# Second norm of a long single-core kernel: turns of the tokens directly behind the modulation's picks, rounding tile by tile, and gate rows behind two heads' queries

## What is computed

```python
# first block, 512 tokens
x = x + concat([y_pool, y_mlstm, y_attn]) @ w_out
x = x + mem_cross_attn(rmsnorm(x, norm_mem_g), mem, ca_wq, ca_wkv, ca_wo)   # the second norm; q = hn @ ca_wq, 4 heads of 128
x = x + ec_moe(rmsnorm(x, norm_ffn_g), router_w, expert_w_gu, expert_w_down)
# second block
shift, scale, gate = split((silu(c) @ w_mod + b_mod)[:, None, :], 3)        # "the modulation"
shift_c, scale_c, _ = split(silu(c_ctx) @ w_mod + b_mod, 3)
h  = rmsnorm(x, norm_g) * (1 + scale) + shift
hc = rmsnorm(ctx, norm_g) * (1 + scale_c) + shift_c
...
x = x + gate * y
```

## Time and profile before

| | us |
|---|---|
| median of 3 runs | 1841.17 (1838.69 to 1841.96) |
| the profiled execution's own time | 1843.9 |
| its span, first to last instruction | 1842.0 |
| TensorE busy in the span | 1686.3 (92%) |
| VectorE, ScalarE, GpSimd busy | 585.0, 468.2, 268.5 |
| mean granted clock of TensorE | 0.989 |

### The profile page before, as it was taken

The page is one execution under the profiler, slowest core; times in us unless marked ns, Lnnn a source line. Parts: engine busy times, 40 slices in busy tenths (PEclk is TensorE's granted clock), DMA queues, the critical chain, the costliest instruction groups (busy, mean ns, idle before and its releaser), DMA issues.

```text
span 1842.0 us, 21089 instructions
## 1 busy us (share of the span) xinstructions
PE 1686.3 (92%) x8647; PEld 985.2 (53%) x8647; DVE 585.0 (32%) x1053; ACT 468.2 (25%) x865; POOL 268.5 (15%) x124
## 2 busy tenths in 40 slices
PE   7999999889898898898979979889899999999998
PEld 5897576653342432424324333243485458878876
DVE  4986784440110200202002020020266351260055
ACT  4456625310000100001000010010264432363232
POOL 0004411000000000000000000000140664116470
PEclk9999999989999999999999999999999999999999
DMA  9334045339999999999999999999901005203111
GB/s 334 134 128 126 1 160 234 121 149 430 427 428 428 429 429 428 429 429 429 428 429 428 428 428 430 429 427 429 383 1 46 1 6 121 92 31 113 68 76 46
DMA packets 65594, 484.19 MB, mean 263 GB/s; under 512 B 10268, under 2 KB 17909, under 8 KB 39807
## 3 DMA queue, kind: packets, MB, share of 16 engines
q1 hardware_dynamic: 65535, 483.36, 64.8%
HBM read 480.94 MB, written 2.41 MB: 262 GB/s over the span
## 4 chain that ended last, share of the span: by engine, by line
PE 72%; DMA 17%; DVE 6%; issue 2%; ACT 2%; POOL 0%; DVEq 0%; SPq 0%; ACTq 0%
PE psum L548 24%; PE psum L1859 17%; DMA ring<-in_expert_w_down 14%; PE psum L1879 7%; PE psum L1842 4%; PE psum L1888 3%; PE psum L2831 2%; PE psum L700 2%; PE psum L665 2%; PE psum L678 2%; DMA ring<-in_expert_w_gu 1%; PE psum L2515 1%; PE psum L2490 1%; PE psum L2499 1%; PE psum L864 1%
## 5 line engine op out<-in xcount | busy, mean ns | idle before, releaser
L1859 PE MATMUL psum<-ring,work_area 128*64 128x512 f32 x2048 | 448.3, 594 | 34.9 <-DMA ring<-in_expert_w_gu 27.1
L1859 PEld LDWEIGHTS psum<-ring,work_area 128*64 128x64 f32 x2048 | 147.8, 137 | 328.9 <-issue 276.9
L1879 PE MATMUL psum<-ring,work_area 128*64 128x512 f32 x1024 | 231.4, 606 | 18.1 <-DMA ring<-in_expert_w_down 16.0
L1949 DVE TENSOR_TENSOR work_area<-psum,work_area 128x512 f32<-128x512 f32 x32 | 20.6, 686 | 592.5 <-ACT work_area L1912 592.5
L1879 PEld LDWEIGHTS psum<-ring,work_area 128*64 128x64 f32 x1024 | 74.5, 139 | 163.9 <-issue 142.2
L2102 POOL TENSOR_TENSOR hn<-x_res,ring 128x1024 f32<-128x1024 f32 x3 | 9.0, 3012 | 1025.5 <-DVE x_res L1956 1025.5
L1912 ACT ACTIVATE work_area<-psum 128x512 f32<-128x512 f32 x32 | 17.4, 594 | 484.8 <-PE psum L1859 484.8
L2014 POOL TENSOR_TENSOR block_lo<-ring,part_hi 128x1024 fp32r<-128x1024 f32 x35 | 86.3, 2473 | 141.6 <-ACT part_hi L2007 141.2
L548 PE MATMUL psum<-h_hi,part_hi 128*128 128x512 f32 x240 | 93.7, 391 | 1.0 <-DVE hn L817 1.0
L1956 DVE TENSOR_TENSOR x_res<-psum,x_res 128x512 f32<-128x512 f32 x64 | 44.2, 691 | 156.9 <-PE psum L1888 156.9
L548 PE MATMUL psum<-h_hi,block_lo 128*128 128x512 f32 x240 | 93.4, 389 | 0.0
(11 more groups left out here) (485 smaller groups left out, 2719.6 us busy)
## 6 DMA issues: line engine op xcount, KB each, us to landing
ring<-in_expert_w_gu SPq DMA_DIRECT2D x128, 2048.0 KB, 27.5
ring<-in_expert_w_down SPq DMA_DIRECT2D x64, 2048.0 KB, 22.4
ring<-in_w_in SPq DMA_DIRECT2D x12, 2048.0 KB, 8.8
extra<-in_w_mod SPq DMA_DIRECT2D x4, 1536.0 KB, 10.6
ring<-in_w_out SPq DMA_DIRECT2D x3, 2048.0 KB, 13.6
ring<-in_ca_wkv SPq DMA_DIRECT2D x2, 2048.0 KB, 12.8
hn<-in_w_mod SPq DMA_DIRECT2D x2, 1536.0 KB, 6.9
x_res<-in_x SPq DMA_DIRECT2D x2, 1024.0 KB, 13.5
```

Of the source, the lines that this page charges most:

```text
L1859: ins = pe.matmul(psum[h * 64:(h + 1) * 64, c, :], xsT[:, k, e * CAP:(e + 1) * CAP], w[:, (2 * c + h) * BANK:(2 * c + h + 1) * BANK], star ...
L1879: ins = pe.matmul(psum[n * 64:(n + 1) * 64, 6, :], hidT[b][:, j, h, :], w[:, j, n * BANK:(n + 1) * BANK], start=(q == 0 and j == 0), stop= ...
```

## The change

Four things move; no operation is added or removed.

1. The gate rows leave their place ahead of the picks. The new `gate_row_pe` stands in `qca_pe` ahead of `ctx_pe`, behind the queries of two heads, and `gate_row_act` stands at the same place of ScalarE's drains.
2. On ScalarE, the rounding of the turned groups of the first tile goes ahead of the sum of squares of the third tile, and that of the second tile ahead of the fourth's.
3. On VectorE, the four rests of these groups go between the fourth tile's additions and its mean.
4. `g_gate_row` is taken from the banks later, so the picks and the turns use other banks, and the context's junk lies where it does not touch the gate's sums.

```diff
@@ add_norm, on_act
                 for t in range(T):
                     if arrived and t % 2 == 0:
                         act.wait_ge(arrived[t // 2], 16)
+                    if t in besides:
+                        besides[t]()
                     for g in groups[2 * t:2 * t + 2]:
                         B.drained(act, g)
                     act.activation(dst[:, t, :], src[:, t, :], ACT.Square, accum_out=ss[:, t:t + 1]).then_inc(squared, 1)
@@ add_norm, on_dve
                         B.release(dve.tensor_tensor(o, B.at(g), o, ALU.add), g)
+                    if t in besides_dve:
+                        besides_dve[t]()
 
                     dve.wait_ge(squared, turn[1] + t + 1)
@@ mod_pe
             pe.wait_ge(mod_added, KD)
-            pe.wait_ge(sem("gate_lin_in"), 16 * 2)
-            for j, g in enumerate(g_gate_row):
-                B.acquire(pe, g)
-                B.filled(product(g, B.at(g), [(ones, mod_total[:, 2 * D + j * BANK:2 * D + (j + 1) * BANK]),
-                                              (ones[0:1, :], gate_lin[j])]), g)
-
             pe.wait_ge(sem("pads"), 4)
...
+        def gate_row_pe():
+            pe.wait_ge(sem("gate_lin_in"), 16 * 2)
+            for j, g in enumerate(g_gate_row):
+                B.acquire(pe, g)
+                B.filled(product(g, B.at(g), [(ones, mod_total[:, 2 * D + j * BANK:2 * D + (j + 1) * BANK]),
+                                              (ones[0:1, :], gate_lin[j])]), g)
+
+        def gate_row_act():
             for j, g in enumerate(g_gate_row):
                 B.full(act, g)
                 B.release(copy(act, gate_row[:, j * BANK:(j + 1) * BANK], B.at(g)), g)
+
+        def mod_act():
             g = g_mod[0]
@@ banks
-        norm2_act, norm2_dve = add_norm(g_out1, x_sb, hn_ca, hn_mem)
-        g_gate_row = B.take(2)
+        norm2_act, norm2_dve = add_norm(g_out1, x_sb, hn_ca, hn_mem, besides={2: lambda: round_h2_act(range(0, 2)), 3: lambda: round_h2_act(range(2, 4))},
+                                        besides_dve={3: lambda: rest_of_h2_dve(range(0, 4))})
         g_mod = B.take(1)
         g_h2 = B.take(KD)
         g_modT = B.take(1)
...
-        ctx_junk = cut(W, 6656, 2, D)
+        ctx_junk = cut(W, 2048, 2, D)
         g_qca = B.take(2)
+        g_gate_row = B.take(2)
         g_ctx = B.take(4)
@@ qca_pe
                 if h == 2:
+                    gate_row_pe()
                     ctx_pe()
@@ qca_drain
                 if h == 2 and eng is act:
+                    gate_row_act()
                     ctx_drain_act()
@@ scalar
             mod_act()
-            round_h2_act()
+            round_h2_act(range(4, KD))
@@ vector
             norm2_dve()
-            rest_of_h2_dve()
+            rest_of_h2_dve(range(4, KD))
```

More of the change, by code:

```diff
@@ L468, in rms_rows, with add_norm @@
             return on_act, on_dve
-        def add_norm(groups, src, dst, mark, arrived=None):
+        def add_norm(groups, src, dst, mark, arrived=None, besides={}, besides_dve={}):
             squared, mean_ready, root_ready = sem("rows_squared"), sem("mean_ready"), sem("root_ready")
@@ L1202, in mod_pe @@
             B.filled(ins, g)
-        def mod_act():
+        def gate_row_pe():
[5 more added lines that the diff above has]
+        def gate_row_act():
             for j, g in enumerate(g_gate_row):
@@ L1581, in build, with round_h2_act, rest_of_h2_dve @@
         four_turns = lambda g: B.at(g).rearrange("p (k c) -> p k c", k=4)
-        def round_h2_act():
-            for i, g in enumerate(g_h2):
+        def round_h2_act(groups):
+            for i in groups:
+                g = g_h2[i]
                 B.full(act, g)
                 act.activation(tile_of(hq_hi, i), four_turns(g), ACT.Identity).then_inc(hT_rounded, 1)
-        def rest_of_h2_dve():
-            for i, g in enumerate(g_h2):
+        def rest_of_h2_dve(groups):
+            for i in groups:
+                g = g_h2[i]
                 dve.wait_ge(hT_rounded, T + i + 1)
```

## The result

The changed kernel is slower: 1847.16 us median against 1842.09 (14 runs each), a ratio of 1.0026 with a 95% interval of 1.0019 to 1.0032, or 4.8 us (0.0026 times 1842; the interval is 3.5 to 5.9 us). The forecast was 6.5 us more than a median of 1841.17 from three executions, which makes 1847.7; with 14 executions the median of before is 0.9 us higher. So the forecast time is met, but the forecast difference lies above the interval. The profiled execution has a span of 1845.3 us against 1842.0.

What follows compares the result with a forecast made beforehand. TensorE, busy 1686.3 of 1842.0 us, was taken to bound the kernel. Gate rows 4.1, terms 2 to 4 together 1.6 and clock 0.8 made +6.5 us, from 1841.2 to 1847.7; range 1843.6 to 1850.6.

Steps and rivals of the forecast that it cites:

- Term 1: Gate rows among queries and context turns, where TensorE has no idle time to cover them: +4.1 us.
- Term 2: In the norm, ScalarE's early roundings wait for TensorE's turns, delaying the third tile's squares: +3.6 us.
- Term 3: On VectorE, four rests stand ahead of the fourth tile's mean and delay it: +1.1 us.
- Term 4: The tail from the fourth tile's scaling to the first query shortens from 6.91 to 3.85 us: -3.0 us.
- Term 5: TensorE's clock low in holes: turns lose 0.8 us, queries lose 1.6 as before; +0.8, bounds -1.6 and +2.6.
- The terms past the stage: Behind the queries, the experts' stage starts later by the queries' delay, keeps its length and absorbs nothing.
- the last query "6 to 7 us later": Sign that the forecast is right: TensorE's last query before attention ends 6 to 7 us later.
- That the clock is low between and behind the holes: Expected low TensorE clock inside holes of 2.4, 4 and 1.4 us around the later tiles' turns.
- the dearer clock (1849.5): Rival: clock low through all turns and the queries' first 6.5 us, +8.3 us; chance 0.14.
- The first case of the rival within 0.2%: Low clock wholly in the holes, turns at full speed: +4.1 us; whole rival, no change to be told, chance 0.13.
- The one in which the early rests close the hole for nothing: Another case within 0.2%: hole ahead of queries closed, -2.4, beside gate rows +4.1: +1.7 us; whole rival's chance 0.13.

Runs made afterwards that it cites:

- e8: The reordered version (e4) with both gate rows moved behind two heads' queries; 1845.19 us against 1842.06 before, ratio 1.0020.
- e4: Changed kernel reordered: picks behind two tiles' turns, gate rows in TensorE's holes, four roundings before the fourth tile's squares, two early rests; 1838.59 us against 1842.17 before.
- e9: The reordered version (e4) with the gate rows and their copies left out altogether; 1839.00 us against 1842.44 before, ratio 0.9978.
- e2: Changed kernel with all four early roundings ahead of the fourth tile's squares, none ahead of the third's; 1842.94 us against 1842.17 before, ratio 1.0005.
- e1: Changed kernel with roundings and rests put back behind the fourth tile, so only the gate rows moved; 1845.98 us against 1842.17 before, ratio 1.0019.
- e12: Second profile of the unchanged kernel before; first query at 24.19 us and last drain at 49.61 us from the norm's first addition.
- e7: Changed kernel with the gate rows back in their old place ahead of the picks, roundings and rests still early; 1847.91 us against 1842.06 before.
- e3: Changed kernel with the gate rows in the holes behind the second and third tiles' turns; 1847.75 us against 1842.17 before, ratio 1.0032.
- e5: As e3, but ScalarE copies the picks ahead of the fourth tile's squares, removing a bank wait; 1843.88 us against 1842.06 before, ratio 1.0011.

## Why the prediction was right, by its own steps

The direction was right, and so was the place. The time (1847.16 for 1847.7) is nearer than the sum deserves: the difference is 4.8 us (3.5 to 5.9) where 6.5 were forecast, and a median of before that is 0.9 us higher than the three executions had it hides about half of that. In the profiled pair the last drain moved by 4.67 us, which can be set against the terms (against the second profile of before it is 3.3, with 0.7 in place of 2.2 for terms 2 to 4).

- **Term 1, gate rows, +4.1:** 4.11 (300.33 to 304.44), with nothing idle around them. e8 against e4, and the free gate rows of e4 against e9, show that it is the place and not the products.
- **Term 2, ScalarE's wait, +3.6:** 3.68 (13.84 against 10.16 from the norm's start). e2 takes it away alone and the first query comes 3.9 earlier.
- **Term 3, rests ahead of the mean, +1.1:** the scaling is 4.70 late (20.51 against 15.81 from the norm's start), less 3.68 leaves 1.02.
- **Term 4, the tail, -3.0:** 4.39 us (284.98 to 289.37) against 6.91, so -2.5. In it are the slow turns of term 5, for which I had put 0.8; they cost some 0.5 (4.39 less the 3.85 worked out).
- **Term 5, the clock, +0.8:** this term was mis-sized. I put 0.8 for the turns and left the queries' loss at 1.6. The turns did run at half clock, but the low stretch ended as the queries began (27.99 us with 4.11 of gate rows, 23.88 without, against 25.50 before): -1.6 for the queries and +0.5 for the turns, -1.1 in all, inside the bounds of -1.6 and +2.6. This accounts for the whole gap between 6.5 and 4.7: 4.1 for the gate rows, 2.2 for terms 2 to 4 with their slow turns, and -1.6 for the queries make 4.7.

One premise was wrong, though the sum did not rest on it: that the gate rows cost nothing in their old place because the other engines' chain passes them by. The chain of the kernel before (start, us, what) runs through their copies:

```profile
279.69 0.20 ACT small L488
279.89 0.98 ACT work_area L426 x2
280.87 0.48 ACT ring L426
281.35 0.50 ACT hq_hi L1586
281.85 0.02 issue
281.87 4.89 DVE hq_lo L1591 x8
```

The 0.98 us of copies stand between the fourth root and the roundings, and the rests and the first query hang on these; TensorE would not have let them start sooner either: its turns begin at 280.49, behind its own gate rows, which by the 0.69 us from a group's turns to ScalarE's reading puts the first rounding at 281.2. e1 measures it: the first query comes 1.0 us earlier without them. In the sum this gain sits in term 4, whose tail was worked out with the copies gone. So moving the gate rows alone costs 4.1 less 1.0, and e1 has 3.5 us (1.8 to 5.2).

The terms past the stage held too: 81.98 and 81.94 us up to the gather, an experts' stage of the same length. Of the signs, the last query "6 to 7 us later" came out at 4.8, for the same reason. That the clock is low between and behind the holes was right. What stays open is how often the clock falls inside the queries of either kernel: there are two profiles of each, which is too few.

Of the rivals, the dearer clock (1849.5) did not come: the queries ran at 1.00. The first case of the rival within 0.2% came by half: the low stretch fell ahead of the queries, as there, but the turns were slow all the same, and what was left, 4.8 us, stood clear of the noise. The one in which the early rests close the hole for nothing did not come, since ScalarE's wait was real; e4 shows what it would have needed: turns ahead of the picks, roundings only in ScalarE's gap, two rests only.

## What to carry to other kernels

Work is done early for nothing only in a gap of its own engine, and only if its input exists by the start of that gap: ask what the input waits for before placing it inside a chain. Work that nobody waits for belongs into a hole of the bounding engine, cut to the hole's length, and never into a stretch without one; here the same 4.1 us of products cost nothing that the medians can tell, or 4.1 (5.8 with the clock). When a group changes its place, follow its buffer as well: two of the experiments lost 2 us or more to a bank whose reader stood late in another engine's program.

## What the runs showed of the hardware that was not expected

- TensorE's clock fell to half (0.52 and 0.53 in the windows of e12 and e1, 0.52 in e7 from 276.76 to 280.31) right behind the float32 gate rows, while TensorE was busy without a hole for more than 10 us. These are three of the nine profiles that have the four products in one stretch; in the other six they were followed by the full clock (the changed kernel, 289.37 to 317.33 at 1.00). What decides is open.
- Two such products take 2.0 us at full clock (279.19 to the next start at 281.19 in e4; half of the 4.11 for four is 2.05) and 3.98 at half (e3), 3.85 in e5; eight turns 0.93 and 1.76 us (281.19 to 282.12 in e4, 285.79 to 287.55 in the changed kernel). How much of it reaches the first query differs: 0.5 of the 0.83 us in the changed kernel, and in e12, where picks and first turns were slow, all of the 1.5.
- Medians of one kernel from 14 to 29 executions lay within 0.4 us (before: 1842.09, 1842.17, 1842.06, 1842.44), but single executions spread over 6 to 9 us (1837.18 to 1846.05 in the widest set), so that one profiled execution can lie 4.6 us off its kernel's median.
